# Grouped register reads, sliced input loads and a divided decay in a one-core layer step

## The chip, the cores and the metric

The kernel runs on one core of one Trainium2 chip. The metric is the device time of one execution in microseconds (us), read as a median over runs. Engine names are those of the profile: PE is TensorE's matmul side, PEld its weight loads, DVE is VectorE, ACT ScalarE, POOL GpSimd, and SP (SPq in the rows) SyncE, which here only issues DMAs.

## The reference

One transformer layer in fp32 on 1024 prompt tokens and 8 sample tokens of width 1024, cut to what the change touches:

```python
z = einsum('btd,de->bte', x, w_in) + b_in        # 4104 columns: q k v o, 4+4 gates, hq hf hi hgt
h, C, n, m = _mlstm(q, k, v, li, lf, C0, n0, m0)  # gates li, lf from the 4+4 gate columns
o_h, S = _hgrn2(silu(hq), k_h, hi, lf_h, S0)      # k_h, lf_h from hf
x = layer_norm(ALPHA * x + concat(h, o_h) @ w_out)
# experts: 4 groups of 4, each token goes to 2 experts of one group
gate = softmax weights of the 2 chosen experts
y = sum over experts of (silu(x @ w1) * (x @ w3) * gate) @ w2
out = layer_norm(ALPHA * x + y)
```

The prompt starts from zero states; the samples each bring their own C (4 heads of 128x128) and S (the same), and one token updates them: new state = decay x old state + outer product of key and value. All new states are outputs.

## The kernel before, in words

All 1032 token columns stand in SBUF as `xT` (128 partitions, 8 slices k of the width, 1032 tokens). The program is written by hand: five engine queues in fixed order, joined by semaphores. `link` and `tell` make an engine wait for its own last instruction.

**Start.** SP loads the gate columns `wgt` (64 wide), then `xT` in three pieces of 344 tokens (each piece all eight k), then the weight groups of `w_in`, 2 MB each, into three slots; ACT's queue loads `params`, `consts` and the masks. PE then works by `project(idx, ...)` (L1556 on, matmul in L1566): eight matmuls over k of one 128-column unit with one 344-token piece, into one of four PSUM banks; bank reuse waits on `proj_read` from ACT. The first three calls are the gates (`wgt`, 64 columns), then come 16 units of 128 columns (hf, hq, q, k; three pieces each). ACT evacuates every piece (L1675 gates, L1690 units) and turns the gates into logarithms, DVE runs the prefix scans on them, and PE spreads the results at unit 3 (L1582 to L1588). A matmul of fp32 stands as two records in the trace.

**Mixer.** Lines 1596 to 1658 are the chunk loop of the first half of the heads, lines 591 to 667 that of the second half together with the output projection.

**Sample states.** After the chunks, `tensor_rest` (L690 to L735) handles the eight samples. PE computes q times the old states; then POOL multiplies each whole state by its decay (L904: C0, then S0, 4096 elements per partition each), while DVE goes through a chain of some forty 128x32 operations (L1080 to L1105) towards the samples' outputs. After that PE makes 16 outer products (L722), ACT copies each into one of three buffers (L746), and POOL adds each to its piece of 512 elements of the state (L908, `add_outer`): twelve here, four in the expert stage. In the same stretch DVE works out the routing of the 1032 tokens (L1381 to L1466): two experts each, sorted by expert into tiles of 32 rows. `tile_expert` says which expert each of 80 tiles needs, `tile_new` whether that differs from the tile before.

**Experts.** 20 steps of four streams: in each step each stream handles one tile of 32 rows, on four column tiles of PE side by side. PE's order in step n is: gate product (L1256), up product (L1261), transpose of the gathered rows of step n+1 (L1224), down product of step n-1 (L1239), transpose of the hidden rows (L1270). SP keeps the weights coming: the loop in `sync_moe` reads each stream's expert and its flag from SBUF into registers, and issues a DMA of 1 MB with `cond=new`, which is issued in any case and moves data only where the expert changed:

```python
if not (last and i == 1):
    coming = [(q, expert_of(q, n + 1), is_new(q, n + 1)) for q in range(STREAMS)]
    sp.wait_ge(s.gate_done, pair * 2 + (i + 1))
    for q, expert, new in coming:
        load_gate(q, expert, new)
    sp.wait_ge(s.up_done, pair * 2 + (i + 1))
    for q, expert, new in coming:
        load_up(q, expert, new)
if not is_first(pair, i):
    coming = [(q, expert_of(q, n), is_new(q, n)) for q in range(STREAMS)]
    sp.wait_ge(s.down_done, n)
```

`expert_of` is line 1154, `is_new` line 1157; gate, up and down loads are issued from lines 1145, 1148 and 1151, the store of the finished rows from line 1176. POOL gathers the rows of each step (L1339). At the end POOL adds each token's two rows (L1356) and the layer norm follows.

## Time and profile before

| | us |
|---|---|
| median of 3 runs (lowest to highest) | 1312.76 (1311.31 to 1315.89) |
| the profiled execution | 1309.31 |
| its span, first to last instruction | 1307.5 |
| PE busy | 1076.3 (82%) |
| DVE busy | 592.1 (45%) |
| start and unit products, 0 to about 255 | 255 |
| mixer chunks, to about 755 | 500 |
| sample states and routing, to the first expert product | 146 |
| expert steps, to the last product | 336 |
| sum of rows, norm and output | 70 |

The profile is of one execution, which took 3.5 us less than the median. Engine shares are averages over stages with different limits, so each stage is read by itself: which wait ends last there.

### The profile page before, as it was taken

Reading aid. Unit: us, or ns where it says so; the run is one execution under the profiler, and the core shown is the slowest. Engines: PE = TensorE matmul, PEld = TensorE weight load, DVE = VectorE, ACT = ScalarE, POOL = GpSimd, SP = SyncE. Lnnn points to the kernel's source line nnn. Section 1 sums busy time; section 2 is a strip of 40 time slices with the busy share of each in tenths; the row PEclk is TensorE's granted clock in tenths of the full one; section 3 lists DMA queues with packets and bytes.
Section 4 is the critical chain, followed back from the end, with each engine's and each line's share of the span. In section 5 each row is a group of like instructions: output and inputs, shape, how many; then the busy total and the mean of one; then the engine's idle time right before and its main releaser. Section 6 shows DMA issues by size and latency. Waiting matters only on the chain.

```text
span 1307.5 us, 18523 instructions
## 1 busy us (share of the span) xinstructions
PE 1076.3 (82%) x6770; PEld 639.2 (49%) x6770; DVE 592.1 (45%) x962; ACT 276.9 (21%) x611; POOL 289.8 (22%) x248
## 2 busy tenths in 40 slices
PE   5999999799999789999999985647867888878500
PEld 2666666556555455656666545324433444434200
DVE  1422133457677567878777756580101111111036
ACT  2442112111211222223322213411000010110013
POOL 0000000001110333445434315222000231200075
PEclk9999999999999889999999978656889998999755
DMA  9220103120000700000010031039687563737496
GB/s 295 90 48 17 65 1 65 28 40 2 1 0 10 260 1 1 33 33 19 15 34 33 33 145 41 28 136 425 238 322 257 192 209 138 279 115 278 154 198 191
DMA packets 38281, 145.96 MB, mean 112 GB/s; under 512 B 5402, under 2 KB 8730, under 8 KB 30154
## 3 DMA queue, kind: packets, MB, share of 16 engines
q1 hardware_dynamic: 32250, 120.73, 26.8%
q0 software_dynamic: 5248, 18.94, 5.7%
q10 hardware_dynamic: 720, 5.47, 1.1%
q8 instruction: 37, 0.61, 0.2%
q14 instruction: 26, 0.21, 0.0%
HBM read 313.23 MB, written 23.79 MB: 258 GB/s over the span
## 4 chain that ended last, share of the span: by engine, by line
PE 62%; SPq 14%; DVE 8%; issue 7%; DMA 7%; POOL 1%; ACT 1%; DVEq 0%; ACTq 0%; POOLq 0%
PE psum L1566 17%; PE psum L608 9%; PE psum L591 9%; PE psum L1596 8%; SPq L1157 4%; SPq L1154 4%; PE psum L627 4%; DMA x_cm<-y_slots,hg_k 2%; PE psum L1256 2%; PE psum L1261 2%; DMA weight_slots<-in_w_in 2%; SPq L1151 1%; DMA hg_decay<-in_w_up 1%; SPq L1145 1%; PE psum L693 1%
## 5 line engine op out<-in xcount | busy, mean ns | idle before, releaser
L1566 PE MATMUL psum<-x_cm,weight_slots 128*128 128x344 f32 x768 | 222.6, 453 | 2.6 <-DMA weight_slots<-in_w_in 2.6
L1566 PEld LDWEIGHTS psum<-x_cm,weight_slots 128*128 128x128 f32 x768 | 145.8, 190 | 78.9 <-DMA weight_slots<-in_w_in 3.2
L1256 PE MATMUL psum<-weight_slots,scratch 128*32 128x256 f32 x1280 | 90.2, 444 | 46.9 <-DMA weight_slots<-in_w_gate 30.9
L1596 PE MATMUL psum<-weight_slots,x_cm 128*128 128x512 f32 x256 | 113.2, 595 | 0.0
L1491 DVE SCALAR_TENSOR_TENSOR scratch<-scratch,psum 128x256 f32<-128x256 f32 x20 | 9.6, 481 | 196.5 <-PE psum L1261 196.5
L1239 PE MATMUL psum<-conv_qk,scratch 128*32 128x512 f32 x320 | 78.0, 632 | 17.0 <-DMA hg_q<-in_w_down 9.6
L1256 PEld LDWEIGHTS psum<-weight_slots,scratch 128*32 128x32 f32 x1280 | 46.6, 127 | 84.3 <-issue 33.0
L1261 PE MATMUL psum<-conv_qk,scratch 128*32 128x256 f32 x640 | 74.2, 385 | 5.7 <-DMA hg_decay<-in_w_up 5.7
L1339 POOL DMA_INDIRECT scratch<-x_rows,hg_k x20 | 19.9, 996 | 265.2 <-PE psum L1224 245.2
L1239 PE MATMUL psum<-hg_k,scratch 128*32 128x512 f32 x160 | 77.9, 633 | 0.0
L1239 PE MATMUL psum<-hg_q,scratch 128*32 128x512 f32 x160 | 77.9, 633 | 0.0
L1596 PEld LDWEIGHTS psum<-weight_slots,x_cm 128*128 128x128 f32 x256 | 47.8, 192 | 54.0 <-issue 54.0
L1261 PE MATMUL psum<-hg_decay,scratch 128*32 128x256 f32 x640 | 74.2, 385 | 0.0
L883 POOL TENSOR_TENSOR scratch<-scratch,hg_k 128x256 f32<-128x256 f32 x56 | 45.9, 820 | 126.0 <-ACT scratch L779 125.9
L1756 POOL TENSOR_TENSOR scratch<-scratch,constants 128x512 f32<-128x512 f32 x8 | 10.1, 1268 | 286.2 <-ACT scratch L1732 286.2
L627 PEld LDWEIGHTS psum<-scratch 128*128 128x128 f32 x448 | 60.2, 198 | 25.4 <-issue 24.2
L627 PE MATMUL psum<-scratch 128*128 128x128 f32 x448 | 61.2, 282 | 3.2 <-POOL scratch L883 3.2
L779 ACT ACTIVATE scratch<-scratch 128x512 f32<-128x512 f32 x56 | 35.3, 630 | 129.3 <-DVE scratch L968 129.2
L608 PE MATMUL psum<-weight_slots,conv_qk 128*128 128x512 f32 x128 | 59.7, 611 | 1.0 <-ACT hg_q L773 1.0
L591 PE MATMUL psum<-weight_slots,x_cm 128*128 128x512 f32 x128 | 59.1, 605 | 0.0
L591 PE MATMUL psum<-conv_qk,x_cm 128*128 128x512 f32 x128 | 57.6, 592 | 0.0
L608 PE MATMUL psum<-weight_slots,hg_q 128*128 128x512 f32 x128 | 57.6, 592 | 0.0
(362 smaller groups left out, 1741.9 us busy)
## 6 DMA issues: line engine op xcount, KB each, us to landing
weight_slots<-in_w_gate SPq DMA_DIRECT2D x80, 1024.0 KB
conv_qk<-in_w_up SPq DMA_DIRECT2D x40, 1024.0 KB
hg_decay<-in_w_up SPq DMA_DIRECT2D x40, 1024.0 KB
conv_qk<-in_w_down SPq DMA_DIRECT2D x40, 1024.0 KB
hg_k<-in_w_down SPq DMA_DIRECT2D x20, 1024.0 KB
hg_q<-in_w_down SPq DMA_DIRECT2D x20, 1024.0 KB
weight_slots<-in_w_in SPq DMA_DIRECT2D x7, 2048.0 KB, 16.6
y_slots<-scratch SPq DMA_DIRECT2D x20, 512.0 KB, 6.0
```

The source lines that it names most:

```text
L591: i = mm(PS[:, bank, :], xT[:, k, c * P:(c + 1) * P], w_slot(g)[:, k, :], start=(k == 0), stop=(k == KD - 1))
L608: i = mm(PS[:, 6 + n, :], lhs, w_out[:, e, n * 512:(n + 1) * 512], start=(e == 0), stop=(e == 7))
L627: i = mm(hp(2 + n % 2, h), xl[:, h], xl[:, h], start=True, stop=True)
L779: tell(A(xlev[n % 2], xlev[n % 2], ACT.Exp), s.level_exp)
L883: tell(g.tensor_tensor(x, x, y, ALU.mult), s.level_scaled)
L1154: return sp.value_load(tile_expert[0:1, bass.ds(n + q * STEPS, 1)].bitcast(I32), min_val=0, max_val=NE - 1)
L1157: return sp.value_load(tile_new[0:1, bass.ds(n + q * STEPS, 1)], min_val=0, max_val=1)
L1239: m = mm(PS[lane, 5 + half, :], hidT[:, k, lane], w_down[q][:, k, half * 512:(half + 1) * 512], start=(k == 0), stop=(k == 1))
L1256: m = mm(PS[lane, 2, 0:FF], xgT[i][:, k, lane], w_gate[q][:, k], start=(k == 0), stop=(k == KD - 1))
L1261: m = mm(PS[lane, 3, 0:FF], xgT[i][:, k, lane], w_up[q][:, k], start=(k == 0), stop=(k == KD - 1))
L1566: i = mm(PS[0:m, idx % 4, 0:PIECE], lhs_of(k), xT[:, k, n * PIECE:(n + 1) * PIECE], start=(k == 0), stop=(k == KD - 1))
L1596: i = mm(PS[:, bank, :], xT[:, k, c * P:(c + 1) * P], w_slot(g)[:, k, :], start=(k == 0), stop=(k == KD - 1))
```

## The change

Four things are edited.

1. **Register reads.** DVE writes experts and flags into one table `step_loads`, ordered by step, with the four streams' words side by side (two extra small copies and a fill before `experts_known`). `experts_of` reads four words with one instruction, and without the range check at run time. The order of loads and waits in the loop is the same.
2. **Start.** `xT` comes by eight k slices of 1032 tokens, in the order of use, with the first hf unit (0.5 MB) and `wgt` behind the first slice; `w_in` is laid out by groups on the host, so that each partition reads one contiguous run. `consts` and the masks move from ACT's queue to SP's, behind the hf units. PE runs unit 0 with k outside and the three pieces inside. `wgt` is 32 columns wide, and the gate products run on four column tiles, one for each k modulo 4, into banks 4 to 6; ACT copies the four partial sums out, and a matmul with the 0/1 matrix `fold` adds them (after the first piece of unit 1). The gates' spreading on PE moves from unit 3 to unit 4.
3. **Decay.** `decay_state(m)` multiplies one sixteenth of the states. POOL runs it for m = 0 to 11 each just ahead of `add_outer(m)`, and then for 12 to 15.
4. Some semaphores are shared to stay within the number there is (`AFTER_FIRST`).

```diff
-        for kind in range(2):
-            state, decay = ((C0, T[9]), (S0, TH[14]))[kind]
-            pool.wait_ge(s.dots, kind + 1)
-            pool.wait_ge(s.kv_in, kind + 1)
-            link(g.tensor_tensor(state, state, decay.unsqueeze(2).to_broadcast([P, HB, P]), ALU.mult))
+        def decay_state(m):
+            kind, heads = m // 8, slice(4 * (m % 8), 4 * (m % 8) + 4)
+            part = (C0, S0)[kind][:, heads, :]
+            decay = (T[9], TH[14])[kind][:, heads]
+            if m % 8 == 0:
+                pool.wait_ge(s.dots, kind + 1)
+                pool.wait_ge(s.kv_in, kind + 1)
+            link(g.tensor_tensor(part, part, decay.unsqueeze(2).to_broadcast([P, 4, P]), ALU.mult))
+
         def add_outer(m):
             part = (C0, S0)[m // 8][:, 4 * (m % 8):4 * (m % 8) + 4, :]
             pool.wait_ge(s.outer_read, m + 1)
             tell(g.tensor_tensor(part, part, kv_outer[m % 3].rearrange("p (a v) -> p a v", a=4), ALU.add), s.state_added)
 
         for m in range(12):
+            decay_state(m)
             add_outer(m)
+        for m in range(12, 16):
+            decay_state(m)
         pool_moe(pool, link, tell, add_outer)
...
-        def expert_of(q, n):
-            return sp.value_load(tile_expert[0:1, bass.ds(n + q * STEPS, 1)].bitcast(I32), min_val=0, max_val=NE - 1)
-
-        def is_new(q, n):
-            return sp.value_load(tile_new[0:1, bass.ds(n + q * STEPS, 1)], min_val=0, max_val=1)
+        def experts_of(n):
+
+            def words(w, top):
+                row = step_loads[0:1, bass.ds((n * 2 + w) * STREAMS, STREAMS)]
+                return nc.values_load_multi_w_load_instructions(row, engines=[mybir.EngineType.SP], min_val=0, max_val=top,
+                                                                skip_runtime_bounds_check_because="experts are minima with NE - 1, flags come from a comparison")[1]
+
+            experts, flags = words(0, NE - 1), words(1, 1)
+            return [(q, experts[q], flags[q]) for q in range(STREAMS)]
...
-                coming = [(q, expert_of(q, n + 1), is_new(q, n + 1)) for q in range(STREAMS)]
+                coming = experts_of(n + 1)
...
-                coming = [(q, expert_of(q, n), is_new(q, n)) for q in range(STREAMS)]
+                coming = experts_of(n)
...
+        by_step = step_loads.rearrange("p (n w q) -> p w q n", w=2, q=STREAMS)
+        link(v.memset(tile_new, 1.0))
         link(v.tensor_tensor(tile_new[:, 1:], tile_e[:, 1:], tile_e[:, 0:TILES - 1], ALU.not_equal))
-        tell(v.tensor_copy(tile_expert.bitcast(I32), tile_e), s.experts_known)
+        link(v.tensor_copy(by_step[:, 1], tile_new.rearrange("p (q n) -> p q n", q=STREAMS)))
+        tell(v.tensor_copy(by_step[:, 0], tile_e.rearrange("p (q n) -> p q n", q=STREAMS)), s.experts_known)
...
-        sp.dma_start(wgt, t["wg"]).then_inc(s.wg_in, 16)
-        for n in range(3):
-            piece = slice(n * PIECE, (n + 1) * PIECE)
-            sp.dma_start(xT[:, :, piece], t["xT"][:, :, piece]).then_inc((s.x_in0, s.x_in1, s.x_in2)[n], 16)
-        for g in range(7):
+        for n, ks in enumerate(X_LOADS):
+            for k in ks:
+                sp.dma_start(xT[:, k], t["xT"][:, k]).then_inc(x_sems[n], 16)
+            if n == 0:
+                sp.dma_start(hf_units[:, 0], w_units[:, 0]).then_inc(s.x_in0, 16)
+                sp.dma_start(wgt, t["wg"]).then_inc(s.x_in0, 16)
+        sp.dma_start(hf_units[:, 1:4], w_units[:, 1:4]).then_inc(s.w_in0, 16)
+        sp.dma_start(cst[:, :], t["consts"]).then_inc(s.consts_in, 16)
+        sp.dma_start(SC[:, 7680:9216], t["masks"]).then_inc(s.consts_in, 16)
+        for g in range(1, 7):
...
-            c0 = GROUPS[g][0]
-            sp.dma_start(w_slot(g), w_cols[:, :, c0:c0 + 512]).then_inc(w_sem[g], 16)
+            sp.dma_start(w_slot(g), w_group[g]).then_inc(w_sem[g], 16)
...
-        pe.wait_ge(s.wg_in, 16)
-        for n in range(3):
-            project(n, lambda k: wgt[:, k, :], 64)
-        for u in range(16):
+        def gates_product(ks):
+
+            for n in range(3):
+                for k in ks:
+                    j = k % 4
+                    i = mm(PS[32 * j:32 * j + 32, 4 + n, 0:PIECE], wgt[:, k, :], xT[:, k, n * PIECE:(n + 1) * PIECE],
+                           start=(k < 4), stop=(k >= 4))
+            if ks[-1] == KD - 1:
+                i.then_inc(s.gates_part, 1)
+
+        for load, ks in enumerate(X_LOADS):
+            pe.wait_ge(x_sems[load], 48 if load == 0 else 16 * len(ks))
+            for k in ks:
+                for n in range(3):
+                    i = mm(PS[:, n, 0:PIECE], hf_units[:, 0, k], xT[:, k, n * PIECE:(n + 1) * PIECE], start=(k == 0), stop=(k == KD - 1))
+                    if k == KD - 1:
+                        i.then_inc(s.projected, 1)
+                if k % 4 == 3:
+                    gates_product(range(k - 3, k + 1))
+        for u in range(1, 16):
             g, j = u // 4, u % 4
-            if j == 0:
+            if j == 0 or u == 1:
                 pe.wait_ge(w_sem[g], 16)
-            if u == 3:
-
-                pe.wait_ge(s.consts_in, 32)
+            if u == 4:
+
                 pe.wait_ge(s.gate_rows, 2)
                 for c in range(NCH):
                     i = nc.tensor.transpose(PS[:, 4 + c // 4, (c % 4) * 96:(c % 4 + 1) * 96],
@@ -1588,7 +1631,13 @@
                     i = mm(PS[:, 6, 64 + h * 24:64 + (h + 1) * 24], sel[0:H, h, :], gs_rows[0:H, :], start=True, stop=True)
                 i.then_inc(s.gates_spread, 1)
             for n in range(3):
-                project(3 + 3 * u + n, lambda k: w_slot(g)[:, k, j * P:(j + 1) * P], P)
+                project(3 * u + n, lambda k: hf_units[:, j, k] if g == 0 else w_slot(g)[:, k, j * P:(j + 1) * P], P)
+                if u == 1 and n == 0:
+                    pe.wait_ge(s.consts_in, 32)
+                    pe.wait_ge(s.gates_copied, 3)
+                    for m in range(3):
+                        i = mm(PS[0:64, 4 + m, 0:PIECE], const("fold"), gates_sum[:, m * PIECE:(m + 1) * PIECE], start=True, stop=True)
+                    i.then_inc(s.gates_part, 1)
 
...
-        act.dma_start(cst[:, :], t["consts"]).then_inc(s.consts_in, 16)
-        act.dma_start(SC[:, 7680:9216], t["masks"]).then_inc(s.consts_in, 16)
         act.wait_ge(s.params_in, 16)
 
         nc.scalar.preload_act_table_set("natural_log_exp_and_others")
-        for idx in range(3):
-            act.wait_ge(s.projected, idx + 1)
-            tell(A(grow[0:64, idx * PIECE:(idx + 1) * PIECE], PS[0:64, idx % 4, 0:PIECE], ACT.Identity,
-              bias=bg[0:64]), s.proj_read)
-        act.wait_ge(s.proj_read, 3)
-        act.wait_ge(s.consts_in, 32)
-        link(A(fr, grow[32:32 + H], ACT.Copy))
-        link(A(lnr, fr, ACT.Abs))
-        link(A(lnr, lnr, ACT.Exp, scale=-1.0))
-        tell(A(lnr, lnr, ACT.Ln, bias=one_col[0:H]), s.forget_ln)
-
         def read_unit(u, dst):
 
             e = [20, 21, 22, 23, 16, 17, 18, 19, 0, 1, 2, 3, 4, 5, 6, 7][u]
             for n in range(3):
-                idx = 3 + 3 * u + n
+                idx = 3 * u + n
                 act.wait_ge(s.projected, idx + 1)
                 tell(A(dst[:, n * PIECE:(n + 1) * PIECE], PS[:, idx % 4, 0:PIECE], ACT.Identity,
                   bias=b_cm[:, e:e + 1]), s.proj_read)
@@ -1693,11 +1729,25 @@
         for j in range(H):
 
             read_unit(j, K[:, j])
+            if j == 0:
+                act.wait_ge(s.gates_part, 1)
+                for n in range(3):
+                    tell(A(gates_sum[:, n * PIECE:(n + 1) * PIECE], PS[:, 4 + n, 0:PIECE], ACT.Copy), s.gates_copied)
+                act.wait_ge(s.consts_in, 32)
             act.wait_ge(s.proj_read, last_piece(j))
             link(A(G[:, j], K[:, j], ACT.Abs))
             link(A(G[:, j], G[:, j], ACT.Exp, scale=-1.0))
             tell(A(G[:, j], G[:, j], ACT.Ln, bias=one_col), s.hf_ln)
-            if j == 1:
+            if j == 0:
+                act.wait_ge(s.gates_part, 2)
+                for n in range(3):
+                    i = A(grow[0:64, n * PIECE:(n + 1) * PIECE], PS[0:64, 4 + n, 0:PIECE], ACT.Identity, bias=bg[0:64])
+                link(i)
+                link(A(fr, grow[32:32 + H], ACT.Copy))
+                link(A(lnr, fr, ACT.Abs))
+                link(A(lnr, lnr, ACT.Exp, scale=-1.0))
+                tell(A(lnr, lnr, ACT.Ln, bias=one_col[0:H]), s.forget_ln)
+            if j == 2:
...
-    wg = np.zeros((D, 64), np.float32)
-    wg[:, 0:H], wg[:, 32:32 + H] = w[:, 2048:2048 + H], w[:, 2048 + H:COL_HG]
+    wg = np.zeros((D, 32), np.float32)
+    wg[:, 0:2 * H] = w[:, 2048:COL_HG]
+    w_groups = [w[:, c:c + 512].reshape(P, KD, 512) for c in (COL_HF, COL_HQ, COL_Q, COL_K, COL_V, COL_O, COL_GT, COL_HI)]
+    w_groups[0] = w_groups[0].reshape(P, KD, 4, P).transpose(0, 2, 1, 3)
```

SP in the loop of the expert steps, before: the reads for gate and up of step n+1 (each TENSOR_LOAD reads one word).

```order
L1154 TENSOR_LOAD hg_k
L1154 ISA x2
L1157 ISA
L1157 TENSOR_LOAD hg_k
L1157 ISA x2
L1154 ISA
L1154 TENSOR_LOAD hg_k
L1154 ISA x2
L1157 ISA
L1157 TENSOR_LOAD hg_k
```

The same place after the change (L1175 is the read, L1163 the gate loads):

```order
L1175 ISA
L1175 TENSOR_LOAD hg_k
L1175 ISA
L1175 TENSOR_LOAD hg_k
L1163 ISA [waits gate_done]
L1163 DMA weight_slots<-in_w_gate 128x2048
```

Eight reads of one word with their checks have become two reads of four words; the same holds ahead of the down loads.

PE at the start, before (`scratch` holds the gate columns):

```order
L1566 MATMUL psum<-x_cm,scratch 64x344 [waits x_in0,wg_in]
L1566 MATMUL psum<-x_cm,scratch 64x344 x7
L1566 MATMUL psum<-x_cm,scratch 64x344 [waits x_in1]
L1566 MATMUL psum<-x_cm,scratch 64x344 x7
L1566 MATMUL psum<-x_cm,scratch 64x344 [waits x_in2]
L1566 MATMUL psum<-x_cm,scratch 64x344 x7
L1566 MATMUL psum<-x_cm,weight_slots 128x344 [waits w_in0]
```

and after the change (L1612 is unit 0, L1603 the gates on column tiles, L1594 the later units, L1639 the fold):

```order
L1612 MATMUL psum<-x_cm,weight_slots 128x344 [waits x_in2]
L1612 MATMUL psum<-x_cm,weight_slots 128x344 x5
L1603 MATMUL psum<-x_cm,scratch 32x344 x12
L1612 MATMUL psum<-x_cm,weight_slots 128x344 [waits x_in3]
L1612 MATMUL psum<-x_cm,weight_slots 128x344 x5
L1612 MATMUL psum<-x_cm,weight_slots 128x344 [waits x_in4]
L1612 MATMUL psum<-x_cm,weight_slots 128x344 x5
L1603 MATMUL psum<-x_cm,scratch 32x344 x12
L1594 MATMUL psum<-x_cm,weight_slots 128x344 [waits w_in0]
L1594 MATMUL psum<-x_cm,weight_slots 128x344 x7
L1639 MATMUL psum<-scratch,constants 64x344 [waits gates_copied,consts_in]
```

The 24 gate matmuls of 64 columns ahead of unit 0 are gone; 24 of 32 columns stand inside unit 0, and three more behind the first piece of unit 1.

POOL at the sample states, before and after (L904 and L918 decay, L908 and L923 additions):

```order
L904 TENSOR_TENSOR x_cm<-x_cm,scratch 128x4096 [waits kv_in,dots,x1_ready]
L904 TENSOR_TENSOR weight_slots<-weight_slots,scratch 128x4096 [waits kv_in,dots,pool_step]
L908 TENSOR_TENSOR x_cm<-x_cm,scratch 128x512 [waits outer_read,pool_step]
L908 TENSOR_TENSOR x_cm<-x_cm,scratch 128x512 [waits outer_read,state_added] x7
L908 TENSOR_TENSOR weight_slots<-weight_slots,scratch 128x512 [waits outer_read,state_added] x4
```

```order
L918 TENSOR_TENSOR x_cm<-x_cm,scratch 128x512 [waits kv_in,dots,x1_ready]
L923 TENSOR_TENSOR x_cm<-x_cm,scratch 128x512 [waits outer_read,pool_step]
L918 TENSOR_TENSOR x_cm<-x_cm,scratch 128x512 [waits state_added]
L923 TENSOR_TENSOR x_cm<-x_cm,scratch 128x512 [waits outer_read,pool_step]
L918 TENSOR_TENSOR x_cm<-x_cm,scratch 128x512 [waits state_added]
L923 TENSOR_TENSOR x_cm<-x_cm,scratch 128x512 [waits outer_read,pool_step]
```

Only the first piece of the decay now stands ahead of the wait for the outer products; the other fifteen stand behind it.

## Rows read from the trace of the kernel before

**Rows 1.** The page: the chain that ended last, by engine and by line.
```profile
PE 62%; SPq 14%; DVE 8%; issue 7%; DMA 7%; POOL 1%; ACT 1%; DVEq 0%; ACTq 0%; POOLq 0%
PE psum L1566 17%; PE psum L608 9%; PE psum L591 9%; PE psum L1596 8%; SPq L1157 4%; SPq L1154 4%; PE psum L627 4%; DMA x_cm<-y_slots,hg_k 2%; PE psum L1256 2%; PE psum L1261 2%; DMA weight_slots<-in_w_in 2%; SPq L1151 1%; DMA hg_decay<-in_
```
**Rows 2.** Busy time of each engine in three stretches (from:to, length; x is instructions).
```profile
0.00:30.00 30.00, 16.54 (x51) 7.71 (x52) 3.05 (x8) 5.53 (x7) 1.23 (x5) 1.00 0.97 285
...
880.00:900.00 20.00, 16.76 (x52) 11.60 (x52) 0.36 (x2) 2.45 (x5) 7.60 (x8) 0.50 1.00 415
...
1143.80:1155.90 12.10, 12.10 (x171) 6.28 (x170) 2.19 (x4) 1.53 (x4) 1.19 (x2) 1.00 0.23 81
```
**Rows 3.** Timeline of SyncE's queue, one step of the experts: start us, us, instruction.
```profile
1077.22 1.15 SPq L1145 DMA_DIRECT2D weight_slots<-in_w_gate  x4
...
1078.80 0.24 SPq L1148 DMA_DIRECT2D hg_decay<-in_w_up  x2
1084.58 0.43 SPq L1151 DMA_DIRECT2D conv_qk<-in_w_down  x2
...
1086.03 0.36 SPq L1176 DMA_DIRECT2D y_slots<-scratch  x1
1092.43 1.41 SPq L1145 DMA_DIRECT2D weight_slots<-in_w_gate  x4
```
**Rows 4.** Lines 1154 and 1157, 1070.9 to 1086.4 us: duration ns min/median/max.
```profile
L1154 SPq TENSOR_LOAD <-hg_k x8: 262/264/687, 1071.0 to 1083.1; - x8
...
L1157 SPq TENSOR_LOAD <-hg_k x8: 263/265/440, 1071.9 to 1083.8; - x8
```
**Rows 5.** Waits of PE, 900 to 1235 us: us in total, times, longest.
```profile
PE psum L1256 <- DMA weight_slots<-in_w_gate: 30.9, 8, 9.4
PE psum L1256 <- issue: 14.9, 3, 8.5
PE psum L1239 <- DMA hg_q<-in_w_down: 9.6, 3, 6.1
PE psum L1239 <- issue: 7.4, 5, 3.1
PE psum L1261 <- DMA hg_decay<-in_w_up: 5.7, 4, 3.1
```
**Rows 6.** The chain that ended last, in order of time: start us, us, what.
```profile
7.65 21.46 DMA weight_slots<-in_w_in
...
900.76 5.77 PE psum L1256 x64
...
960.84 11.43 DMA weight_slots<-in_w_gate
972.32 5.83 PE psum L1256 x64
...
1212.53 5.19 PE psum L1256 x64
```
**Rows 7.** Timeline of PE at the start.
```profile
10.90 15.69 PE L1566 MATMUL psum<-x_cm,scratch 128*64 128x344 f32 x48 [10.90 <-DMA x_cm<-in_xT]
...
29.15 41.04 PE L1566 MATMUL psum<-x_cm,weight_slots 128*128 128x344 f32 x141 [2.55 <-DMA weight_slots<-in_w_in]
```
**Rows 8.** Timelines of POOL, DVE and PE, 800 to 822 us.
```profile
805.24 7.03 POOL L904 TENSOR_TENSOR x_cm<-x_cm,scratch 128x4096 f32<-128x4096 f32 x1 [6.92 <-PE psum L701]
...
805.66 6.65 DVE L1082 TENSOR_TENSOR scratch<-scratch 128x32 f32<-128x32 f32 x1
...
812.57 6.90 DVE L1084 TENSOR_TENSOR scratch<-scratch 128x32 f32<-128x32 f32 x1
...
821.49 0.64 PE L704 MATMUL psum<-scratch,constants 128*128 128x32 f32 x2 [13.22 <-DVE scratch L1092]
```
**Rows 9.** Timelines of POOL and DVE in the routing, 861 to 864 us.
```profile
861.13 1.26 POOL L908 TENSOR_TENSOR x_cm<-x_cm,scratch 128x512 f32<-128x512 f32 x1 [4.67 <-ACT scratch L746]
...
861.17 1.25 DVE L1425 TENSOR_SCALAR hg_decay<-hg_decay 128x16 int32<-128x16 f32 x1
862.46 0.18 DVE L1426 TENSOR_SCALAR hg_decay<-hg_decay 128x16 int32<-128x16 int32 x1
```

More of the change, by code:

```diff
@@ L257, in _program @@
     tile_e = work(TILES)
+    tile_new = work(TILES)
     x1_keep = [XF[:, (c + 4) % 8 * D:((c + 4) % 8 + 1) * D] for c in range(8)] + [SC[:, 8 * D:9 * D]]
@@ L1151, in load_down @@
             sp.dma_start(w_down[q], wd[bass.ds(expert, 1)].rearrange("e p k n -> p (e k) n"), cond=new).then_inc(s.w_down_in, 16)
-        def expert_of(q, n):
-            return sp.value_load(tile_expert[0:1, bass.ds(n + q * STEPS, 1)].bitcast(I32), min_val=0, max_val=NE - 1)
-        def is_new(q, n):
-            return sp.value_load(tile_new[0:1, bass.ds(n + q * STEPS, 1)], min_val=0, max_val=1)
+        def experts_of(n):
[5 more added lines that the diff above has]
+            return [(q, experts[q], flags[q]) for q in range(STREAMS)]
         sp.wait_ge(s.experts_known, 1)
         sp.wait_ge(s.mixed, NTT)
-        first = [expert_of(q, 0) for q in range(STREAMS)]
-        for q in range(STREAMS):
-            load_gate(q, first[q], None)
+        first = experts_of(0)
+        for q, expert, _ in first:
+            load_gate(q, expert, None)
         sp.wait_ge(s.outer, 8)
-        for q in range(STREAMS):
-            load_up(q, first[q], None)
+        for q, expert, _ in first:
+            load_up(q, expert, None)
         sp.wait_ge(s.slots, 1)
-        for q in (2, 3, 0, 1):
-            if q == 0:
-                sp.wait_ge(s.outer, 16)
-            load_down(q, first[q], None)
+        for q, expert, _ in first[2:]:
+            load_down(q, expert, None)
+        sp.wait_ge(s.outer, 16)
+        for q, expert, _ in first[:2]:
+            load_down(q, expert, None)
         early_outs.append(outs[0])
@@ L1913, in layouts @@
         "x": x,
-        "w_in": w,
-        "wg": wg.reshape(P, KD, 64),
+        "w_in": np.stack([v.reshape(P, KD * 512) for v in w_groups]),
+        "wg": wg.reshape(P, KD, 32),
         "params": np.concatenate([v.reshape(P, -1) for v in params], 1),
```

37 lines of the change are left out of this document (22 added, 15 removed).

## The prediction

> **What bounds the kernel now.** I read the chain of waits first, then each stage. The chain [rows 1] is PE for 62%, which says that most of the span is matmuls behind matmuls that the change does not touch. But 14% of it, some 180 us, is SyncE's queue, and its lines are 1154 and 1157, the register reads. They are all in the expert stage. So there are three places to price: the start, where PE waits for loads; the sample states; and the expert steps.
>
> *Experts.* The reader should see a queue with no idle time in the timeline of SP [rows 3]. From one gate load to the next, 1077.22 to 1092.43, a step takes 15.2 us. Between the last up load (ends 1079.04) and the first down load (1084.58) lie 5.5 us, and between the store (ends 1086.39) and the next gate load 6.0 us: 11.5 us of sixteen one-word reads, 0.72 us each with their address arithmetic and checks, of which the read itself is 0.26 [rows 4]. The remaining 3.7 us are DMA issues. PE could be faster than that: in 1143.80 to 1155.90, one step from its gate to its last transpose, PE is busy 12.10 of 12.10 us [rows 2]. The stage runs from the gate product of step 0 at 900.76 to that of step 19 at 1212.53 [rows 6], 311.8 us or 16.4 a step, against 19 x 12.1 = 230. Of the 82 us between, PE's waits hold 68.5 [rows 5]; the rest is matmuls at the lower clock behind a wait (the gate product takes 5.83 us after the wait that ends at 972.32 [rows 6], in a step that holds five such groups in 12.1 at the higher one). Waits put down to a DMA count as SP's too where the DMA was issued late.
>
> *Start.* PE has 15.69 us of gate matmuls from 10.90 us on, then waits for the first weight group until 29.15 [rows 7], a load issued at 7.65 that took 21.5 us [rows 6] in a stretch where the queues were full at 285 GB/s; wider loads reach 415 [rows 2].
>
> *Sample states.* PE waits 13.22 us for DVE, which has two 128x32 operations of 6.65 and 6.90 us, exactly as long as POOL is in its decay of 7.03 us each [rows 8]. A small one beside no POOL work takes 0.18 [rows 9].
>
> **The change part by part.**
>
> *Register reads.* Sixteen reads become four of four words. No row shows a four-word read. From below it costs what one word costs without checks, 0.26 plus some issue, say 0.35 us. From above it costs four whole reads, 4 x 0.72 = 2.9 us. I take 0.8 us, nearer the low end, because it is one instruction with one address and no check. Then SP needs 3.7 + 4 x 0.8 = 6.9 us a step, under PE's 12.1, and waits for PE instead. SP stays hidden up to (12.1 - 3.7)/4 = 2.1 us a read. The order of its waits is unchanged, so nothing new queues behind one.
>
> What is late next is weight traffic. Steps 0 to 4 take 972.32 - 900.76 = 71.6 us [rows 6], and most of that stays, since the first loads (12 MB) and two early changes of experts keep the queues full. What goes there is the late issue: the gate loads of step 4, the 11.43 us DMA in [rows 6] that ends the wait at 972.32, stood behind eight reads of 6.0 us by [rows 3]. So 71.6 - 6.0 = 65.6. The other 15 steps need 15 x 12.1 = 181.5 us, and I add 15 for steps in which two streams change experts at once, for the 3 MB that SP puts in ahead of step 19, and for the clock after those waits. Sum 262.1; gain 311.8 - 262.1 = **50 us**. From below: only the waits named "issue" go, 14.9 + 7.4, and the 6 us, which is 28. From above: 65.6 + 181.5 with nothing added, a gain of 65.
>
> *Start.* PE can begin when the first slice, the first unit, the gate columns and `params` are in, 1.3 MB, where before it took 10.90 us for the 2.9 MB it shared the queues with. In proportion that is 4.9 us, and with some 2 us of fixed start that does not shrink, I estimate 6.8. Unit 0 is 48 records; by [rows 7] 141 records take 41.04 us, 0.291 each, but the 48 gate records took 15.69 where 48 x 0.291 is 14.0, so the first of them ran slower, at a cost of 1.7. Unit 0 pays that instead: 15.7 us. The 24 gate matmuls, 48 records on four column tiles side by side (as the expert products run), take 48 x 0.291 / 4 = 3.5 us. Unit 1 can start at 6.8 + 15.7 + 3.5 = 26.0. Before, it started at 29.15 + 48 x 0.291 = 43.1. The fold adds six records, 1.7 us, once. Gain 43.1 - 26.0 - 1.7 = **15.4 us**. Everything up to 255 us is PE behind PE, so it arrives whole. The loads allow this: 4.9 MB up to the last slice at 285 GB/s end near 20 us, and after them PE still has the last two slices and half of the gates, 5.2 us. The fold waits for `consts`, 7.5 MB into the queue, 29 us at that rate, when PE is near the end of the first piece of unit 1 at 30.7. The DVE chain of the gates starts a little later than before, and its reader moves from unit 3 to unit 4, one unit or 14.0 us: hidden. If instead the starved PE stayed slow all through unit 0 and the gates (twice 0.291 a record), it would lose 14 us and the gain would be 1. From above: 17, with the loads at 415 GB/s.
>
> *Decay.* Ahead of DVE's chain only one piece is left, 7.03/8 = 0.88 us. DVE's two operations lose 13.2 us, less that piece: 12.4 gained, and the wait of PE for DVE [rows 8] shrinks by it. But the pieces come back. Pieces 1 to 3 go with the first additions; pieces 4 to 15, twelve, fall into the routing, which is one chain of DVE operations that everything waits for. There an addition of 1.26 us on POOL stretches a DVE operation from 0.18 to 1.25 [rows 9], 0.85 of its length. Twelve pieces of 0.88 to 1.26 us (taken at 0.95) give 12 x 0.95 x 0.85 = 9.7 us. The Trainium skill, page "SBUF — State Buffer", section "SBUF: two separate sides", calls the port pair of VectorE and GpSimd an exclusive lock that the one that starts first keeps for the whole instruction; by that rule alone each piece would cost its full length, 11.4 us in all, and the part would give 1 us instead of 2. The trace agrees with the rule for the operations shown. Two more small DVE operations and a fill before the experts are known cost 0.4. Gain 12.4 - 9.7 - 0.4 = **2 us**; from below -5 (pieces at 1.26 and a DVE operation waiting out each, 15, and more gaps), from above 12.
>
> *Hidden at no cost.* The new layouts of the later weight groups (PE waits for none of them before), and ACT's three copies of gate sums, which lie beside unit 1; were that cover gone they would cost at most what POOL needs for additions of 512 elements [rows 9], 3 x 1.26 = 3.8 us.
>
> *Sum.* 50 + 15.4 + 2 = 67.4 us off the profiled execution's 1309.3, which is 1241.9. The median of the runs before lies 3.5 us over that execution, so I name **1245 us** as the median; the times below hold the same 3.5.
>
> **The rivals.**
>
> *A. Weight traffic, not SP, set the pace.* For it: PE's waits in the experts are put down to DMAs for 46 of 68.5 us [rows 5]. Against it: a DMA issued behind eight reads ends late by those reads, and 19 such delays of up to 6.0 us are in these 46. If all 46 us stay, the experts gain 28, the sum is 45, and the time 1268.
>
> *B. A four-word read costs as four.* At 2.9 us a read SP needs 3.7 + 11.6 = 15.3 us a step, as now. Then the experts gain nothing, the sum is 17, and the time 1296. For it: the read's 0.26 us is less than half of what each costs in the queue, so what stands around it may scale with registers. Against it: the order shows one instruction and no check rows.
>
> *C. Slower than before.* The same place and mechanism, at a price per read over the point where it eats the other gains as well: 17 us over 19 steps is 0.9 a step, so from (15.3 + 0.9 - 3.7)/4 = 3.1 us a read on. At 4 us a read a step takes 19.7 us, 4.4 x 19 = 84 us more, and less the 17 the time would be about 1380. Nothing in the rows speaks for it except that the first reads of a group reach 0.69 us [rows 4].
>
> *D. The start does not overlap.* PE slow throughout and the decay's pieces at their worst: 1 and -5 in place of 17, so the sum is 46 and the time 1267.
>
> **How the numbers follow.** Forecast 0.72, A 0.12, D 0.07, B 0.06, C 0.03. The range reaches from the upper bounds that I find likely (experts 58, start 17, decay 6: 81 off, 1232) to A and D, 1268, and leaves out B, C and part of the tails: the range is asymmetric since losses are likelier than gains beyond the sum. About 0.3%, 4 us, is what a measurement of this kernel can tell from no change. Only C is slower; faster 0.96, same 0.01, slower 0.03.
>
> **What would show it.** Right: unit 1 starting near 26 us; the two DVE operations under 1 us each and PE's wait for DVE at 3 to 4 us; the routing chain on DVE some 10 us longer with POOL's pieces beside it; reads of about 0.8 us in SP's queue and SP waiting for gate products; steps of 12 to 13 us from the fifth on. Wrong: four-word reads over 2 us; DMA waits of PE in the experts that stay at 40 us or more; or unit 1 starting after 30 us.

## The result and the profile after

| | before | after |
|---|---|---|
| median of runs, us | 1314.33 | 1252.59 |
| lowest to highest, 4 runs each | 1311.31 to 1315.89 | 1251.31 to 1253.22 |
| the profiled execution | 1309.31 | 1251.31 |
| its span | 1307.5 | 1249.5 |

The ratio after to before is 0.9532, with a 95% interval from 0.951 to 0.9553: 61.7 us less. The forecast was 1245 us in a range from 1232 to 1268.

The chain that ended last, by engine and by line, now has SyncE at 1% and no register read among its lines, where it had 14% [rows 1]:

```profile
PE 77%; DVE 8%; DMA 8%; issue 3%; POOL 1%; SPq 1%; ACT 1%; DVEq 0%; ACTq 0%; POOLq 0%
PE psum L1594 17%; PE psum L619 9%; PE psum L602 9%; PE psum L1645 9%; PE psum L1279 5%; PE psum L1284 5%; PE psum L1262 4%; PE psum L638 4%; DMA weight_slots<-in_w_gate 2%; DMA x_cm<-y_slots,hg_k 2%; DMA hg_decay<-in_w_up 2%; PE psum L1247 1%; PE psum L1612 1%; PE psum L704 1%; PE psum L577 1%
```

For the ledger four landmarks are enough. In the chain before (start us, us, what) the samples' state products begin, and at [rows 6] the gate products of steps 0 and 19:

```profile
788.26 8.77 PE psum L693 x64
```

The same landmarks in the chain after (L704 is the state product, L715 the product that waits for DVE, L1279 the gate product):

```profile
774.03 8.77 PE psum L704 x64
...
794.56 0.41 PE psum L715 x2
...
882.87 5.90 PE psum L1279 x64
...
933.86 16.48 DMA weight_slots<-in_w_gate
950.38 6.27 PE psum L1279 x64
...
1152.96 5.68 PE psum L1279 x64
```

| stretch | forecast gain | measured gain | from |
|---|---|---|---|
| start to the state products | 15.4 | 14.2 | 788.3, now 774.0 |
| state products to DVE's release of PE | 12.4 | 12.7 | 33.2, now 20.5 |
| from there to gate product 0 | -10.1 | -9.0 | 79.3, now 88.3 |
| gate product 0 to gate product 19 | 50 | 41.7 | 311.8, now 270.1 |
| behind gate product 19 | 0 | -1.5 | 95.0, now 96.5 |
| sum | 67.4 | 58.0 | span 1307.5, now 1249.5 |

**Start.** PE's timeline (start, us, instructions, and in brackets its idle time before and what ended it) answers to [rows 7]:

```profile
6.66 8.96 PE L1612 MATMUL psum<-x_cm,weight_slots 128*128 128x344 f32 x24 [6.66 <-DMA scratch<-in_wg]
...
24.56 1.94 PE L1603 MATMUL psum<-x_cm,scratch 128*32 128x344 f32 x24
26.44 4.89 PE L1594 MATMUL psum<-x_cm,weight_slots 128*128 128x344 f32 x16
31.26 1.95 PE L1639 MATMUL psum<-scratch,constants 128*64 128x344 f32 x6
```

PE begins at 6.66 and waits for nothing from there on up to 50 us. The gates take 1.95 us twice (the rows left out are the first of these pieces and the second half of unit 0, 7.21 us), unit 1 begins at 26.44, and the fold takes 1.9.

**Decay.** The timelines of POOL, DVE and PE answer to [rows 8]; beside the first piece one DVE operation takes 0.67 us instead of 6.65, and PE waits 0.52 us for DVE instead of 13.22 (and 2.93 before it for ACT, as it did under cover of the longer wait):

```profile
791.00 1.04 POOL L918 TENSOR_TENSOR x_cm<-x_cm,scratch 128x512 f32<-128x512 f32 x1 [7.11 <-issue]
...
791.20 0.19 DVE L1099 TENSOR_TENSOR scratch<-psum,scratch 128x32 f32<-128x32 f32 x1
791.43 0.67 DVE L1100 TENSOR_TENSOR scratch<-scratch 128x32 f32<-128x32 f32 x1
...
793.80 0.24 PE L712 MATMUL psum<-constants,scratch 32*128 32x32 f32 x1 [2.93 <-ACT scratch L856]
794.56 0.41 PE L715 MATMUL psum<-scratch,constants 128*128 128x32 f32 x2 [0.52 <-DVE scratch L1110]
```

L1099, which reads one of its inputs from PSUM, starts 0.2 us behind the piece and isn't stretched.

In the routing it is paid back. POOL has a piece and an addition in turn, and some of DVE's operations end when POOL's do; this stretch answers to [rows 9]:

```profile
846.23 1.06 POOL L918 TENSOR_TENSOR weight_slots<-weight_slots,scratch 128x512 f32<-128x512 f32 x1
847.37 1.28 POOL L923 TENSOR_TENSOR weight_slots<-weight_slots,scratch 128x512 f32<-128x512 f32 x1
...
846.43 0.90 DVE L1460 TENSOR_SCALAR hg_k<-hg_k 128x18 int32<-128x18 int32 x1
...
847.57 1.12 DVE L1462 CAST hg_k<-hg_k 128x18 f32<-128x18 int32 x1
```

L1460 starts 0.2 us behind the piece and ends at 847.33, 0.04 behind the piece; L1462 starts 0.2 behind the addition and ends at 848.69, 0.04 behind it. Not every operation is held. A reduction and a reciprocal that start beside an addition run at their own length:

```profile
823.26 1.26 POOL L923 TENSOR_TENSOR x_cm<-x_cm,scratch 128x512 f32<-128x512 f32 x1
...
823.27 0.19 DVE L1414 TENSOR_REDUCE hg_decay<-hg_decay 128x9 f32<-128x36 f32 x1
823.50 0.21 DVE L1415 RECIPROCAL hg_decay<-hg_decay 128x9 f32<-128x9 f32 x1
```

**Experts.** SyncE's queue from the store to the next gate loads, as in [rows 3], and line 1175, the four-word reads, between 1099.8 and 1126 us, as in [rows 4] (ns min/median/max):

```profile
1111.01 0.36 SPq L1199 DMA_DIRECT2D y_slots<-scratch  x1
1113.60 1.41 SPq L1163 DMA_DIRECT2D weight_slots<-in_w_gate  x4
```

```profile
L1175 SPq TENSOR_LOAD <-hg_k x9: 295/298/887, 1099.9 to 1124.1; - x9
```

Between the store's end (1111.37) and the gate loads lie 2.2 us instead of 6.0, though one of the two reads there is slow (0.84). The median four-word read takes 0.298 us where a one-word read took 0.264. PE's waits from 880 to 1180 us (in total, times, longest) answer to [rows 5]:

```profile
PE psum L1279 <- DMA weight_slots<-in_w_gate: 13.3, 2, 9.6
PE psum L1279 <- issue: 9.9, 2, 6.8
PE psum L1262 <- DMA hg_q<-in_w_down: 6.8, 2, 6.3
PE psum L1284 <- DMA hg_decay<-in_w_up: 5.5, 2, 3.4
...
PE psum L1262 <- issue: 3.1, 4, 1.0
```

The waits for weights and for issue are 38.6 us instead of 68.5. What is left stands in few steps: between gate products, step 2 takes 17.5 us, step 3 22.5, step 5 17.0 and the last one 19.0, while seven steps take 12.1 to 12.2, which is PE alone.

### The profile page after: what moved, and what is told of

Its sections match the earlier page's. It is cut to its first block, busy times and chain, and to the rows that moved or that the text cites. A ratio compares the mean times of both kernels' runs of the same rounds, so it can differ in the third digit from the quotient of the medians.

```text
span 1249.5 us, 17577 instructions
## 1 busy us (share of the span) xinstructions
PE 1057.5 (85%) x6776; PEld 632.3 (51%) x6776; DVE 588.0 (47%) x964; ACT 278.0 (22%) x614; POOL 292.5 (23%) x262
## 4 chain that ended last, share of the span: by engine, by line
PE 77%; DVE 8%; DMA 8%; issue 3%; POOL 1%; SPq 1%; ACT 1%; DVEq 0%; ACTq 0%; POOLq 0%
PE psum L1594 17%; PE psum L619 9%; PE psum L602 9%; PE psum L1645 9%; PE psum L1279 5%; PE psum L1284 5%; PE psum L1262 4%; PE psum L638 4%; DMA weight_slots<-in_w_gate 2%; DMA x_cm<-y_slots,hg_k 2%; DMA hg_decay<-in_w_up 2%; PE psum L1247 1%; PE psum L1612 1%; PE psum L704 1%; PE psum L577 1%
## 5 line engine op out<-in xcount | busy, mean ns | idle before, releaser
L1594 PE MATMUL psum<-x_cm,weight_slots 128*128 128x344 f32 x720 | 209.0, 453 | 0.0
L1594 PEld LDWEIGHTS psum<-x_cm,weight_slots 128*128 128x128 f32 x720 | 136.6, 190 | 71.9 <-issue 1.1
L1279 PE MATMUL psum<-weight_slots,scratch 128*32 128x256 f32 x1280 | 83.5, 419 | 24.1 <-DMA weight_slots<-in_w_gate 13.3
L1262 PE MATMUL psum<-conv_qk,scratch 128*32 128x512 f32 x320 | 75.2, 613 | 9.8 <-DMA hg_q<-in_w_down 6.8
L1262 PE MATMUL psum<-hg_k,scratch 128*32 128x512 f32 x160 | 75.0, 613 | 0.0
L1262 PE MATMUL psum<-hg_q,scratch 128*32 128x512 f32 x160 | 75.0, 613 | 0.0
L1279 PEld LDWEIGHTS psum<-weight_slots,scratch 128*32 128x32 f32 x1280 | 44.0, 120 | 56.9 <-issue 20.4
L1863 DVE TENSOR_SCALAR scratch<-scratch,small 128x1024 f32<-128x1024 f32 x8 | 6.5, 814 | 114.9 <-ACT scratch L1726 114.9
```

The source lines that it names most:

```text
L1262: m = mm(PS[lane, 5 + half, :], hidT[:, k, lane], w_down[q][:, k, half * 512:(half + 1) * 512], start=(k == 0), stop=(k == 1))
L1279: m = mm(PS[lane, 2, 0:FF], xgT[i][:, k, lane], w_gate[q][:, k], start=(k == 0), stop=(k == KD - 1))
L1594: i = mm(PS[0:m, idx % 4, 0:PIECE], lhs_of(k), xT[:, k, n * PIECE:(n + 1) * PIECE], start=(k == 0), stop=(k == KD - 1))
```

## The experiments

All are made from the changed kernel, and each median is of four runs. The kernel before ran beside each group of them, with medians from 1313.7 to 1314.3 us; the changed kernel did not run again, so a difference from its 1252.59 is between runs that were not side by side.

### The checked one-word reads put back

```diff
...
-                row = step_loads[0:1, bass.ds((n * 2 + w) * STREAMS, STREAMS)]
-                return nc.values_load_multi_w_load_instructions(row, ..., skip_runtime_bounds_check_because=...)[1]
+                return sp.value_load(step_loads[0:1, bass.ds((n * 2 + w) * STREAMS + q, 1)], min_val=0, max_val=top)
...
```

> The changed kernel with its register reads undone alone: sixteen one-word reads a step with their range checks, from the new table. Theory (SyncE's queue set the pace of the expert stage): a step is again no shorter than 15.2 us of SyncE, the stage from the gate product of step 0 to that of step 19 goes from 270.1 back to about 312 us, and the time is 1252.6 + 42 = 1294 us. Rival (weight traffic set the pace, and the stage is shorter for another reason): the stage stays within 5 us of 270 and the time within 5 us of 1252.6.

Measured: 1297.91 us, 45.3 over the changed kernel; the stage is 315.6 us and no wait of SyncE for PE is left from 1020 to 1140 us, where the changed kernel has 54. The reads are worth 45.3 us, 3.9 more than expected, and weight traffic did not set the pace: the rival falls. The stage is 3.8 us longer than in the kernel before; one profile each doesn't tell whether that is scatter.

### One-word reads without the check

The same edit, with the changed kernel's read call and its skipped check for each single word.

> The changed kernel with sixteen one-word reads a step, as before, but without the range check. Theory (what made a read cost 0.72 us was the check and its address arithmetic around a read of 0.26): SyncE needs 16 x 0.40 + 3.7 = 10.1 us a step, under PE's 12.1, and the stage grows only where gate loads are issued about 1 us later, at most 11 steps that change an expert: 1253 to 1263 us. Rival (the count of read instructions is what costs, and grouping by four is what helped): as with checks, near 1294 us.

Measured: 1255.81 us, 3.2 over the changed kernel and 42.1 under the one with checks. Its stage is 274.9 us, 4.8 longer than the changed kernel's. The reads' line in the kernel with checks (1100 to 1132 us) and in the one without (1100 to 1126 us; ns min/median/max):

```profile
L1174 SPq FUSED_REGOPS  x57: 46/147/172, 1099.9 to 1131.8; - x57
L1174 SPq SEQ_ASSERT  x32: 18/18/18, 1100.1 to 1131.3; - x32
L1174 SPq TENSOR_LOAD <-hg_k x32: 262/270/795, 1100.3 to 1131.5; - x32
```

```profile
L1175 SPq TENSOR_LOAD <-hg_k x36: 262/270/880, 1099.8 to 1125.2; - x36
L1175 SPq FUSED_REGOPS  x27: 46/46/84, 1100.1 to 1125.0; - x27
```

The read is the same 0.27 us. What is gone is the check behind it: a register operation of 0.147 us, an assertion, and the issue gaps around them. In the traces, 1020 to 1140 us, a read and what stands around it take 0.67 us of the queue on average with the check and 0.41 without. Eight unchecked reads behind the up loads go by in 2.3 or 3.2 us, where checked ones take 4.4 or 5.3; behind the store they take 3.1 to 4.4. SyncE fits under PE again:

```profile
SPq L1169 <- PE psum L1261: 7.2, 6, 1.7
SPq L1166 <- PE psum L1283: 5.8, 1, 5.8
```

These waits, 1020 to 1140 us, are 13 us against 54: it fits, but barely. **Dropping the check is worth 42.1 of the 45.3 us, grouping the words by four another 3.2**, about the size of what two medians of four runs can tell apart, though every run of the one is slower than every run of the other, and the stages differ.

### The whole decay put back

```diff
-        for m in range(12):
-            decay_state(m)
-            add_outer(m)
-        for m in range(12, 16):
-            decay_state(m)
+        for kind in range(2):
...
+            link(g.tensor_tensor(state, state, decay.unsqueeze(2).to_broadcast([P, HB, P]), ALU.mult))
...
+        for m in range(12):
+            add_outer(m)
```

> The changed kernel with the decay undone alone: POOL multiplies each state whole, ahead of all additions. Theory (pieces cost DVE their length in the routing): PE's wait for DVE before L715 is 13 us again, a loss of 12.7, and the chain from the mixer's last product to the tables is shorter by the pieces' part of the 9.7 us that it grew, some 9.2. Net 3 to 4 us slower, 1256 us. Rival (the chain grew for another reason, such as the new table's copies or additions at another time): only the 12.7 show, 1265 us. Second rival (the pieces cost more than they give): faster than 1252.6.

Measured: 1255.85 us, 3.3 slower. Both halves show. PE's wait is 13.21 us again:

```profile
791.89 7.03 POOL L915 TENSOR_TENSOR x_cm<-x_cm,scratch 128x4096 f32<-128x4096 f32 x1 [6.96 <-PE psum L712]
...
792.31 6.66 DVE L1094 TENSOR_TENSOR scratch<-scratch 128x32 f32<-128x32 f32 x1
...
808.13 0.64 PE L715 MATMUL psum<-scratch,constants 128*128 128x32 f32 x2 [13.21 <-DVE scratch L1104]
```

and from there to gate product 0, at 888.22, it is 80.1 us instead of 88.3. So the pieces cost 8.2 us of that stretch, and the division is worth the rest, 4.5 us in the profiles. Fifteen pieces lie in the stretch: 0.55 us each, or 0.7 if only the twelve in the routing are counted. The kernel before needed 79.3 us there, so 0.8 of the 9.0 lost are not the pieces; the new table's copies lie there, but weren't tried alone.

### The start alone

The checked reads and the whole decay put back at once leave the start changed against the kernel before, and with it the new table of experts and flags and the shared semaphores.

> The changed kernel with reads and decay both undone, so that only the start is changed against the kernel before. Theory: the start is worth the 14.2 us by which the state products began earlier, all of it arriving at the end, so 1314.3 - 14.2 = 1300 us. The three parts then add up to the whole within 3 us. Rival (a start that is earlier meets something later, or the stages are not independent): more than 5 us away from 1300.

Measured: 1304.45 against 1314.24 for the kernel before on the same chip, ratio 0.993 (0.9909 to 0.9951), so 9.8 us with 6.4 to 12 in the interval. 14.2 is outside. In its profile the state products begin at 776.03, 12.2 us earlier than before; unit 1 begins at 27.47 there, and in the profiles of the kernels with this start anywhere from 26.44 to 27.57. Its span is only 7.8 us shorter: 4.4 of the 12.2 are lost behind it, 0.7 up to gate product 0, 1.6 in a stage of 313.3 us and 2.1 in an end behind gate product 19 of 97.1. The edit touches neither stage nor end. The end was 95.0 in the one profile of the kernel before and 95.0 to 97.3 in the eleven with this start, in ten of them about 96 or more; why was not looked for. In the same eleven the state products begin at 774.0 to 776.5, and the changed kernel's 774.0 is the earliest: a lucky draw. By runs the start is worth about 10 us, 12 at most.

By medians the parts are 9.8 for the start (1314.24 to 1304.45), 6.5 for the decay on top of it (to 1297.91) and 45.3 for the reads (to 1252.59). Steps of one path add up to the whole by construction, so this doesn't show that the parts are independent. Taken off the changed kernel alone the decay gave 3.3 and not 6.5, and 9.8 + 3.3 + 45.3 is 3.3 short of the 61.7. The stretch from the state products to gate product 0 shrinks by 4.3 us in one pair of profiles and by 4.5 in the other, so nothing in that stretch speaks for two different prices.

### The decay where DVE idles

DVE has little to do from 795 to 807 us, while PE makes the samples' output products, and none from 862 to 870.

```diff
+        pool.wait_ge(s.sq_in, 2)
         for m in range(12):
             decay_state(m)
+        for m in range(12):
             add_outer(m)
+        pool.wait_ge(s.onehots, 1)
         for m in range(12, 16):
             decay_state(m)
```

> The changed kernel with the sixteen decay pieces at other times: twelve in one run behind DVE's L1114 (795.2 us), where DVE has little to do until 807.1 while PE makes the samples' output products, and the last four behind the onehot matrices, where DVE waits 8 us for PE. Theory (a piece costs only where it lies beside DVE's chain): PE's wait ahead of L715 stays short, and from the end of the samples' products to gate product 0 it is 67 to 69 us instead of 76.3: 7.5 to 9 us faster than the changed kernel, 1244 to 1245 us. Rival (twelve pieces in a row hold up the five small DVE operations L1119 to L1123 for which PE waits): L725 starts 3 to 5 us later and eats half of it, 1248 us. Second rival (the additions and not the pieces are what stretches the chain): no change, 1252.6 us.

Measured: 1241.36 us, 11.2 faster than the changed kernel, and more than expected. Its gate product 0 begins at 873.48, 9.4 us earlier; the other 1.8 are within the scatter of start and end told above. POOL's and DVE's timelines:

```profile
795.30 8.99 POOL L918 TENSOR_TENSOR x_cm<-x_cm,scratch 128x512 f32<-128x512 f32 x8 [10.82 <-DVE scratch L1117]
804.37 4.40 POOL L918 TENSOR_TENSOR weight_slots<-weight_slots,scratch 128x512 f32<-128x512 f32 x4
...
797.77 0.91 DVE L1122 TENSOR_TENSOR small<-scratch 128x32 f32<-128x32 f32 x1 [1.15 <-ACT scratch L852]
...
798.95 0.92 DVE L1126 TENSOR_TENSOR small<-small 128x32 f32<-128x32 f32 x1
```

Three of the five small operations are stretched, yet PE reaches its product at 800.67, as it did at 801.20. The rival (they would hold PE up) and the second one (only the additions stretch the chain) fall. From the end of the samples' products to gate product 0 it is 66.6 us, against 75.9 in the changed kernel and 67 to 69 expected.

### The kept rows loaded later

The wait that ends with gate product 4 is 16.48 us of DMA in the chain above. I had blamed late issue. But in the changed kernel those gate loads go out 4.2 us behind gate product 3 instead of 9.9, and product 4 follows after 22.5 us instead of 22.7. Ahead of them in the queue are 2 MB of kept rows, issued at 929.97. (Not shown here: SyncE's loop starts two pairs later.)

```diff
-            if isinstance(pair, int) and n == 2:
+            if isinstance(pair, int) and n == 6:
                 sp.wait_ge(s.outputs, 16 * early_outs[0])
                 keep_x1(4)
...
```

> The changed kernel with one load moved: the 2 MB of kept rows that SyncE issues at step 2, just ahead of the gate loads of step 4, goes out at step 6 (SyncE's loop starts two pairs later for that). Theory (those loads arrive late because 2 MB are ahead of them, not because they were issued late): step 3 to 4 falls from 22.5 to 16 to 17.5 us and nothing grows by more than 1 us, so 5 to 6 us faster, 1247 us. Rival (late issue, or a total rate that is the limit): step 3 to 4 keeps 21 us or more, or the two steps behind it take the gain back; within 2 us of 1252.6.

Measured: 1253.49 us, no gain. The chain shows why both views held half of the truth:

```profile
927.46 3.63 PE psum L1286 x64
...
933.08 11.12 DMA weight_slots<-in_w_gate
944.24 5.35 PE psum L1286 x64
...
994.84 12.04 DMA weight_slots<-in_w_gate
1006.93 5.31 PE psum L1286 x64
```

Step 3 falls from 22.5 to 16.8 us (927.5 to 944.2), so the 2 MB were what stood in the way. But step 7 grows from 12.9 to 18.0 and step 8 from 12.1 to 13.8: there they stand between the 2 MB of down loads of step 6 and the gate load of step 8.

### The kept rows loaded early

The windows of the changed kernel (from:to, busy times, granted clock, DMA share, GB/s) show queues that move nothing ahead of the first gate loads:

```profile
848.00:852.00 4.00, 0.00 (x0) 0.00 (x0) 3.79 (x7) 0.00 (x0) 3.77 (x4) 0.50 0.00 0
```

```diff
         out_dma(sp, t["out_C_s"].rearrange("p h b v -> p (h b) v"), C0)
+        sp.wait_ge(s.outputs, 16 * outs[0])
+        keep_x1(4)
         sync_moe(sp, keep_x1)
...
                 sp.wait_ge(s.outputs, 16 * early_outs[0])
-                keep_x1(4)
```

> The changed kernel with the 2 MB of kept rows loaded as soon as the store of the first state has landed, near 844 us, where the DMA queues move nothing until the first gate loads of 858. Theory (in late_x1 the gain of 6 us at step 3 was given back at step 7 only because the moved load then stood ahead of others; in an idle stretch it meets none): step 3 to 4 is 16.5 to 17 us, step 4 to 5 13.8, and no other step grows by more than 1 us, so 6 to 7 us faster than the changed kernel, 1246 us. Rival (the total rate in the steps is the limit, so the gain is given back wherever the load goes): within 2 us of 1252.6. Second rival (SyncE's wait for that store delays the first gate loads): gate product 0 comes later than 884 us.

Measured: 1244.92 us, 7.7 faster. The same stretch moves the load now, step 3 takes 17.3 us, and no step grows by more than 1.0. Gate product 0 begins at 884.76, later than the 884 that the second rival named; but the state products begin 1.7 us later too, and the first gate loads as well (859.85 against 858.12), so the wait for the store costs nothing that shows:

```profile
848.00:852.00 4.00, 0.00 (x0) 0.00 (x0) 3.76 (x8) 0.00 (x0) 3.77 (x4) 0.50 0.90 334
```

### The stores of the last pair behind the down loads

```diff
-            if last and i == 0:
-                ...
-                out_dma(sp, t["out_S_s"].rearrange("p h b v -> p (h b) v"), S0)
...
                 for q, expert, new in coming:
                     load_down(q, expert, new)
+                if last and i == 0:
+                    ...
+                    out_dma(sp, t["out_S_s"].rearrange("p h b v -> p (h b) v"), S0)
```

> The changed kernel with the 1 MB norm load and the 2 MB state store of the last pair put behind the down loads of step 18, where they stood ahead of the gate loads of step 19. Theory (those 3 MB are what gate product 19 waits for): the last step falls from 19.0 to 12.2 to 13 us, 6 to 7 us faster, 1246 us. Rival (the 3 MB then delay the last down loads or the gathers of the finished rows instead): the tail behind gate product 19 grows from 96.5 by as much, and the time is within 2 us of 1252.6.

Measured: 1245.90 us, 6.7 faster. Behind gate product 19 the last down product now waits 8.9 us for its load instead of 6.3, as the rival has it, but the whole end is 97.1 us against 96.5, so the rival has little of the gain. The last step is a step of PE alone, 12.1 us:

```profile
1137.01 3.59 PE psum L1279 x64
...
1149.15 3.59 PE psum L1279 x64
```

### Together

First with the late load of the kept rows, run side by side with the single moves:

> All three moves at once. Theory: they lie in three stretches that do not meet, so the gains add: 8 + 5.5 + 6.5 = 20 us off 1252.6, 1232 to 1234 us. Rival (steps that start earlier meet later loads): less than 15 us, 1238 us or more.

Measured: 1237.37 us, 15.2 faster where 20 were expected: what the late load gives at step 3 it takes at steps 7 and 8 (18.8 and 14.6 us). Then with the early load:

> The decay in the gap, the stores of the last pair behind the down loads, and the kept rows early, together. Theory: three stretches that do not meet, 11 + 6.5 + 6.5 = 24 us off 1252.6, 1228 to 1230 us. Rival (with the chain 9 us shorter the idle stretch of the queues is too short for the 2 MB, and the first gate loads or the gather come later): gate product 0 later than 875 us and 1233 us or more.

Measured: **1230.61 us**, 22.0 under the changed kernel and 83.7 under the one before (ratio 0.9361, 0.934 to 0.9381), the fastest of all; gate product 0 begins at 873.55, and the stage is 255.7 us. Alone the three moves gave 11.2 + 7.7 + 6.7 = 25.6; of the 3.6 missing, part may be scatter, and the profiles don't say more: the stage gains 14.4 where the single moves gave 13.6 together. The longest wait left is that of the last down product, behind gate product 19, where the late stores alone left 8.9 us and the changed kernel has 6.3; the two for gate loads end ahead of gate products 4 and 6:

```profile
PE psum L1266 <- DMA hg_q<-in_w_down: 9.1, 1, 9.1
PE psum L1283 <- DMA weight_slots<-in_w_gate: 7.9, 2, 4.6
```

Which steps load new weights depends on the routing, and no other routing was run; the places of the decay and of the early load don't depend on it.

## Why the prediction was right, point by point

**That SyncE's reads bound the experts: right, and shown.** With them back the gain of the stage is gone. The price that I took, 0.8 us a read, was too high: 0.298 is the median, and over 1020 to 1140 us a read takes 0.51 of the queue on average, with one of the first two behind the store often near 0.9. That changed nothing, as SyncE is hidden up to 2.1. Rivals B and C, which need 2.9 and 3.1 us a read, fall. I had put the cost to words and instructions alike; the runs put nearly all of it to the check.

**The experts' 50 us: the right mechanism, too large a size; measured 41.7.** Two terms failed. The first is "what goes there is the late issue", 6.0 us in step 3. Counted from gate product 3 the loads went out 5.7 us earlier and landed 0.3 us earlier, because 2 MB were ahead of them; moving these 2 MB takes 5.2 to 5.7 us off the step. Steps 0 and 1 gave 4.1 instead, so that steps 0 to 4 took 67.5 us against 65.6. The second is the 15 us that I added for later waits: 21.1 were needed (202.6 less 181.5), and 6.9 of them are the last step, where the 3 MB that I named hold up gate product 19. I had named the cause and given it no price of its own.

**Rival A (traffic sets the pace)** is wrong for the stage as a whole, as PE's waits for weights fell from 46.2 to 25.6 us, and right for step 3.

**The start's 15.4: 14.2 in the profile, 9.8 in the runs.** Step by step the timeline agrees: PE from 6.66 (6.8), unit 0 16.0 (15.7), gates 3.8 (3.5), unit 1 at 26.44 (26.0), fold 1.9 (1.7), and no slow unit 0, so that rival D falls. What fell is "it arrives whole": by medians a third is missing. Up to 2.5 us of it is how much the time of the state products varies, and up to 2 may be the longer end; where the rest goes, the profiles don't settle, since the steps vary by as much.

**The decay's 2: 3.7 in the profile, 3.3 in the runs.** Gain 12.7 (12.4), loss 9.0 (10.1). The pieces took 8.2 of it, where I had 9.7, and what else lies in the stretch 0.8, where I had 0.4. What I had wrong is that each piece holds DVE for 0.85 of its length. By the rows above L1460 and L1462 end with POOL's instruction, while L1099, the reduction and the reciprocal run at their own length beside one. The Trainium skill, page "SBUF — State Buffer", section "SBUF: two separate sides", has the exclusive lock for operations of DVE in a two-port mode or with two inputs in SBUF alone; the trace agrees, as L1099 has one input in PSUM, and the reduction and the reciprocal have one input each. My sum took the lock for all operations. How much of the difference that makes was not measured.

**The total** was 7.6 us too low, inside the range. In the profiled execution the sum fell 9.4 us short (58.0 of 67.4): 8.3 in the experts, 1.2 at the start and 1.5 in the end, which I had put at nothing, less what the decay gave over. That the median missed by less is luck: I had allowed 3.5 us between profiled execution and median, and the changed kernel showed 1.3.

## What to carry to other kernels

In this kernel a register read with its range check costs 0.67 us of a queue on average, without it 0.41 for one word and 0.51 for four: where one queue issues everything, price its instructions before blaming the traffic. When a wait is put down to a DMA, compare issue and landing in both kernels: if the issue moves and the landing doesn't, look for the bytes ahead of it, and move them into a stretch where the queues are empty, not merely to a later one. Work of POOL on tiles that DVE doesn't touch can still hold DVE's chain; put it where DVE waits for PE.

## What was not expected of the hardware

- Three more words in a read of registers cost 0.028 us (0.270 to 0.298). The table lies in SBUF; of tables in HBM no run here shows anything.
- POOL's work lengthened L1100 (TENSOR_TENSOR with both inputs in SBUF), L1460 (TENSOR_SCALAR) and L1462 (CAST); a reduction and a reciprocal of 0.2 us beside an addition of 1.26 were not.
- One of the first two reads behind the store of a step often takes 0.84 to 0.89 us, in kernels with one-word and with four-word reads alike, while behind the up loads none takes over 0.31 (1020 to 1140 us). The cause wasn't looked for.
- After the same wait of 2.02 us, the up product of step 13 took 3.66 us in the changed kernel and 5.32 in the one with late stores. The windows show the clock granted at 1.00 (2.4 GHz) in the one and 0.68 on average, so in part at 1.2 GHz, in the other; up to the wait both had 1.00:

```profile
1076.10:1079.70 3.60, 3.60 (x65) 1.98 (x65) 0.00 (x0) 0.00 (x0) 0.00 (x0) 1.00 0.91 319
```

```profile
1077.60:1082.90 5.30, 5.30 (x65) 2.48 (x65) 0.00 (x0) 0.00 (x0) 0.00 (x0) 0.68 0.68 235
```
